# Mixers of the first two token tiles on shared weight loads, and half of the feed-forward weights narrowed by cast transfers inside device memory

## What is computed

```
u = rmsnorm(h); q, f, i, og, xp, ga, gb = split(u @ w_in)          # w_in: 1024 x 6656
o  = hgrn2(q, f, i)            # 8 heads, state 128 x 128 per head, carried along the tokens
ya = (rmsnorm_per_head(o) * sigmoid(og)) @ w_br_hgrn               # 1024 x 1024
yb = pool_mixer(xp) @ w_br_pool                                    # 4 trailing-mean windows, 512 x 1024
h  = h + (sigmoid(ga) * ya + sigmoid(gb) * yb) @ w_out             # 1024 x 1024
u  = rmsnorm(h)
h  = h + (silu(u @ w_ffn_gate) * (u @ w_ffn_up)) @ w_ffn_down      # 1024 x 2816, twice, and 2816 x 1024
return rmsnorm(h)[:, 16:]
```

## Time and profile before

| | |
|---|---|
| median of 3 runs | 2167.08 us (2166.81 to 2477.38) |
| profiled execution, its own time | 2170.29 us |
| its span on the slowest core, 5 | 2168.7 us (cores 2158.5 to 2168.7) |
| TensorE busy | 2088.9 us, 96% |
| VectorE, ScalarE, GpSimd busy | 1001.8, 1007.0, 574.0 us |
| mean granted TensorE clock | 0.985 to 0.987 of full |
| moved by DMA | 405.24 MB, mean 187 GB/s |

### The profile page before, as it was taken

The page is one execution under the profiler, slowest core; times in us unless marked ns, Lnnn a source line. Parts: engine busy times, 40 slices in busy tenths (PEclk is TensorE's granted clock), DMA queues, the critical chain, the costliest instruction groups (busy, mean ns, idle before and its releaser), DMA issues.

```text
span 2168.7 us, 38075 instructions; the slowest of 8 cores (2158.5 to 2168.7 us)
## 1 busy us (share of the span) xinstructions
PE 2088.9 (96%) x11476; PEld 1106.8 (51%) x11476; DVE 1001.8 (46%) x1756; ACT 1007.0 (46%) x1492; POOL 574.0 (26%) x671
## 2 busy tenths in 40 slices
PE   6777998999999999999999999999999999999997
PEld 3432554555555555555555555555555555554447
DVE  4644453447534742474246523662357235732223
ACT  4832763258415742464247623662358324731111
POOL 3121120001105251423243143314332414223300
PEclk9988999999999999999999999999999999999999
DMA  9999999887565666557555755575557555565577
GB/s 202 211 198 249 217 223 238 228 213 221 147 183 154 186 190 177 158 156 225 170 151 170 223 162 159 168 222 162 166 164 199 180 173 158 165 175 174 169 197 191
DMA packets 232789, 405.24 MB, mean 187 GB/s; under 512 B 24208, under 2 KB 66704, under 8 KB 232592
## 3 DMA queue, kind: packets, MB, share of 16 engines
q1 hardware_dynamic: 210080, 364.62, 57.6%
q0 software_dynamic: 20880, 36.32, 11.7%
q10 hardware_dynamic: 1632, 1.88, 0.4%
HBM read 385.94 MB, written 53.08 MB: 202 GB/s over the span
## 4 chain that ended last, share of the span: by engine, by line
PE 84%; DMA 12%; SPq 1%; issue 1%; DVE 1%; ACT 1%; POOL 0%; DVEq 0%; POOLq 0%; ACTq 0%
PE psa L496 75%; DMA wsc<-wr 6%; DMA wr<-wpk 5%; PE psa L661 5%; DMA wr<-wsc 1%; PE psa L782 1%; SPq L364 1%; PE psa L796 1%; PE psa L815 1%; PE psa L816 1%; PE psa L831 0%; DMA fa<-xT 0%; PE psa L620 0%; PE psa L601 0%; DVE ba L630 0%
## 5 line engine op out<-in xcount | busy, mean ns | idle before, releaser
L496 PE MATMUL psa<-ba,wr 128*128 128x456 bf16 (+2 forms) x8960 | 1776.7, 354 | 19.8 <-DVE ba L546 6.6
L496 PEld LDWEIGHTS psa<-ba,wr 128*128 128x128 bf16 x8960 | 868.1, 98 | 830.2 <-issue 40.6
L906 DVE TENSOR_TENSOR ba<-psa,fa 128x456 bf16<-128x456 f32 (+1 forms) x198 | 124.5, 631 | 250.8 <-PE psa L496 213.0
L905 ACT ACTIVATE fa<-psa 128x456 f32<-128x456 f32 (+1 forms) x198 | 107.1, 551 | 217.1 <-PE psa L496 185.1
L589 POOL TENSOR_TENSOR fa<-fa 128x456 f32<-128x456 f32 (+1 forms) x160 | 158.0, 996 | 161.8 <-DMA fa<-xT 76.9
L773 POOL TENSOR_TENSOR ba<-fa 128x456 bf16<-128x456 f32 (+1 forms) x48 | 61.1, 1272 | 480.7 <-ACT fa L756 257.9
L363 POOL DMA_DIRECT2D wr<-wpk x145 | 76.8, 535 | 373.8 <-DMA wsc<-wr 180.6
L661 PE MATMUL psa<-wr,ba 128*114 128x512 bf16 (+1 forms) x576 | 136.6, 384 | 3.0 <-DMA wr<-wpk 3.0
L765 DVE TENSOR_TENSOR_SCAN fa<-ba,fa 128x456 f32<-128x456 bf16 (+1 forms) x72 | 83.4, 1159 | 120.1 <-ACT fa L763 120.0
L866 POOL TENSOR_TENSOR fa<-fa 128x456 bf16<-128x456 f32 (+1 forms) x48 | 55.3, 1152 | 289.2 <-DVE fa L863 289.2
L863 DVE SCALAR_TENSOR_TENSOR fa<-fa,psa 128x456 f32<-128x456 f32 (+1 forms) x72 | 45.3, 629 | 165.9 <-PE psa L496 165.9
(11 more groups left out here) (84 smaller groups left out, 1767.2 us busy)
## 6 DMA issues: line engine op xcount, KB each, us to landing
wr<-wsc SPq DMA_DIRECT2D x1040, 256.0 KB, 3.0
wr<-wpk POOLq DMA_DIRECT2D x128, 256.0 KB, 14.3
wsc<-wr SPq DMA_DIRECT2D x128, 256.0 KB, 18.3
wr<-wsc SPq DMA_DIRECT2D x72, 192.0 KB, 2.8
fa<-xT SPq DMA_DIRECT2D x6, 1824.0 KB, 13.9
outT<-fa SPq DMA_DIRECT2D x6, 1824.0 KB, 11.0
wr<-wsc SPq DMA_DIRECT2D x72, 128.0 KB, 2.3
fa<-xT SPq DMA_DIRECT2D x2, 1840.0 KB, 13.2
```

Source lines behind the costliest of these rows:

```text
L496: last = e.matmul(ps[bank][:, 0:c1 - c0], lhsT=sl[0].ap(i * 128, (i + 1) * 128), rhs=s_.ap(c0, c1), start=(start and i == 0), stop=(stop a ...
L905: yield act(lambda e: e.activation(out=sg.ap(0, nt), in_=ps[bg][:, 0:nt], func=AF.Silu), [PS(bg)], [sg.rg(0, nt)], tset="S", banks=[bg])
L906: yield dve(lambda e: e.tensor_tensor(out=ACT[fc].ap(0, nt), in0=ps[bu][:, 0:nt], in1=sg.ap(0, nt), op=ALU.mult), [PS(bu), sg.rg(0, nt)], ...
```

## The change

- The first two tiles are one group. Heads go in the order (tile 0, head 0), (tile 1, head 0), (0, 1), (1, 1) and so on; the values, the pooling projection, the merge and `WO` are likewise done for both tiles on one load of each unit (`wkey`, `wdone`: tile 1 uses tile 0's slot and gives it back). Tile 1 thus has no mixer loads of its own. The feed-forward parts stay separate.
- Tile 1's mixer gets buffers of its own (`TWIN`) inside buffers of later stages: its `U` is `U2`, its values and outputs lie in `ACT`, its merged output in `VB`, and a fourth set of head buffers and the pooling scratch lie in the third residual buffer (`HX`). The load of tile 2's input therefore waits for the last head of tile 1, the first feed-forward part for tile 1's merge, tile 2's values for tile 1's `WO`.
- While the group's heads run there are two pairs of PSUM banks for the recurrence (3, 4 and 6, 7) and three dense banks; then banks 3 and 4 become dense.
- Every second feed-forward unit (`DD`, 34 of 68) is narrowed by one DMA from `wpk` straight to `wsc`, issued by GpSimd behind each load from the 19th on, until all 34 are out. In tile 0 these units are then loaded from `wsc` by SyncE and are not written back.
- `master` spawns both feed-forward parts behind the group's merge, then tile 2 and the others as before.

```
+DD = [u for u in range(NU) if WU[u][1] in ("fg", "fu", "fd")][1::2]
+DDI = 1
...
-        free_banks = {b: 0.0 for b in range(NDENSE)}
+        free_banks = {b: 0.0 for b in range(KA2)}
...
+        GROUP = [[(t, h) for h in range(8) for t in (0, 1)]] + [[(t, h) for h in range(8)] for t in range(2, n_tiles)]
+        def wkey(t, name):
+            return (0, name) if t == 1 else (t, name)
+
+        def wdone(t, keys):
+            return () if t == 0 else keys
...
-            if t == 0:
+            if t == 0 and u not in DD:
                 P.emit("pool", lambda e: e.dma_start(out=sbuf, in_=wpk[u, :, 0:n]), ...)
                 pend.append((slot, lambda: P.emit("sp", lambda e: e.dma_start(out=back, in_=sbuf), ...), nissue[0]))
+                if nload[0] % DDI == 0 and nload[0] > NSLOT and ndd[0] < len(DD):
+                    k = ndd[0]
+                    u2 = DD[k]
+                    n2 = WU[u2][4] * WU[u2][5]
+                    ndd[0] += 1
+                    P.emit("pool", lambda e: e.dma_start(out=wsc[u2, :, 0:n2], in_=wpk[u2, :, 0:n2]), w=[(("dr", u2), 0, 1)], sem=f"d{k}", inc=16, dma=True, dur=0.54, xfer=XL)
...
         def s_norm1(t):
-            if t == 1:
-                yield Gate(("hs", 0, 7))
+            if t == 2:
+                yield Gate(("hs", 1, 7))
+                yield Count(("pooled", 0), 4)
+                yield Count(("pooled", 1), 4)
...
+                if t == 2:
+                    yield Count(("res", 1), 8)
...
         def s_head(t, h):
-            s = HS[(h + 1) % HSN]
+            grp, n = HSEQ[(t, h)]
+            KB = KA2 if t < 2 and n % 2 else KA_
+            s = HS[n % 4] if t < 2 else HS[(n + 1) % HSN]
...
-            yield Lock("KA")
+            if t == 1:
+                yield Gate(("hs", 0, h))
+            yield Lock(f"KA{KB}")
...
-        def s_merge(t):
-            yield Count(("head", t), 8)
+        def s_merge(ts):
+            seq = [(t, j) for j in range(8) for t in ts]
+            if len(ts) > 1:
+                seq = sorted(seq, key=lambda x: (x[1] + GAP * x[0], x[0]))
+            yield Gate(("hs", 1, 6)) if len(ts) > 1 else Count(("head", ts[0]), 8)
...
         def s_ffn(t):
-            if t:
-                yield Gate(("downpe", t - 1))
+            yield Gate(("downpe", t - 1) if t else ("mixed", 1))
...
         def master():
+            yield Spawn(1, s_norm1(0))
+            yield Spawn(1, s_norm1(1))
+            yield Spawn(1, s_norm1(2))
+            yield Spawn(0, s_pool1(0))
+            yield Spawn(0, s_pool1(1))
+            yield Spawn(1, s_v([(0, 0), (0, 1), (1, 0), (1, 1)]))
+            for t, h in GROUP[0]:
+                yield Spawn(0, s_head(t, h))
+            yield Spawn(1, s_merge((0, 1)))
+            yield Spawn(5, s_ffn(0))
+            yield Spawn(5, s_ffn(1))
+            for t in range(2, n_tiles):
+                if t >= 3:
+                    yield Gate(("oproj", t - 2))
+                    yield Spawn(1, s_norm1(t))
+                yield Gate(("mixed", t - 1))
...
```

More of the change, by code:

```diff
@@ L24 @@
 LAG = 8
+GAP = 1.5
 PG = 7
@@ L268, in build_nc @@
         semnames += [f"{c}{i}" for c in "wvb" for i in range(NSLOT)]
+        semnames += [f"d{k}" for k in range(len(DD))]
         sems = {n: es.enter_context(nc.semaphore("s_" + n)) for n in semnames}
@@ L280, in build_nc @@
         NH = 3
-        H = [[FA.alloc(NTM) for _ in range(8)] for _ in range(NH)]
-        HALL = [Buf(fa_t, None, h[0].off, 8 * NTM) for h in H]
+        HALL = [FA.alloc(8 * NTM) for _ in range(NH)]
+        H = [[b.sub(j * NTM, NTM) for j in range(8)] for b in HALL]
         CF = FA.alloc(C_TOT)
@@ L524, in prologue @@
                 issue_load(0, u, s)
-            for i in range(HSN):
+            for i in range(HSN + 1):
                 g_(lambda e, i=i: e.memset(HS[i]["QI"].ap(128, 602), 0.0), [HS[i]["QI"].rg(128, 602)], dur=0.3)
@@ L644, in s_norm1 @@
                 yield Count(("u", t - 1), 8)
[L645 to L650, removed]
-            if t:
-                yield Count(("head", t - 1), 8)
-            for hf in range(2):
-                units = [(t, f"WI{hf}{i}") for i in range(4)]
+            yield from norm(t, H[t % NH], P_G1, MB(t).U, RSTD[0], "split" if t <= 1 else "sum" if t >= POOL_FROM else "mm",
+                            apply_gate=Gate(("ufree", 0 if t == 2 else t - 1)) if t >= 2 else None, out_flag="u")
@@ L655, in s_v, with fn @@
+        def s_v(parts):
+            for t, hf in parts:
+                nt = SIZES[t]
+                c = nt // 4
+                U_, V = MB(t).U, MB(t).V
+                yield Count(("u", t), 8)
+                if t == 2:
+                    yield Count(("res", 1), 8)
+                if t >= 3:
+                    yield Count(("head", t - 1), 8)
+                units = [wkey(t, f"WI{hf}{i}") for i in range(4)]
                 for ci in range(4):
                     b = yield Bank()
-                    def fn(e, sl, b=b, ci=ci):
+                    def fn(e, sl, b=b, ci=ci, c=c, U_=U_):
@@ L659, in fn @@
                         last = None
                         for kc in range(8):
-                            last = e.matmul(ps[b][0:c, 0:512], lhsT=U[kc].ap(ci * c, (ci + 1) * c),
+                            last = e.matmul(ps[b][0:c, 0:512], lhsT=U_[kc].ap(ci * c, (ci + 1) * c),
                                             rhs=sl[kc // 2].ap((kc % 2) * 512, (kc % 2) * 512 + 512), start=(kc == 0), stop=(kc == 7))
                         return last
-                    yield Op("pe", fn, [U[kc].rg(0, nt) for kc in range(8)], [PS(b)], 8 * 512 / 2400.0, units=units,
-                             done=units if ci == 3 else ())
+                    yield Op("pe", fn, [U_[kc].rg(0, nt) for kc in range(8)], [PS(b)], 8 * 512 / 2400.0, units=units,
+                             done=wdone(t, units) if ci == 3 else ())
@@ L704, in s_pool1 @@
                 yield dve(lambda e, sw=sw, xp=xp, g=g, w=w: e.scalar_tensor_tensor(
[L705 to L706 removed]
+                    out=YP[g].ap(0, nt), in0=xp.ap(16, end), scalar=-float(w), in1=sw.ap(16, end), op0=ALU.mult, op1=ALU.add),
+                    [xp.rg(16, end), sw.rg(16, end)], [YP[g].rg(0, nt)])
                 if t == 0:
[L708 removed]
+                    tmp = XTMP
                     yield dve(lambda e, sw=sw, g=g: e.tensor_tensor(out=tmp.ap(0, 16), in0=sw.ap(16, 32),
```

232 lines of the change are left out of this document (134 added, 98 removed).

## The result

The changed kernel takes 2191.61 us (2190.59 to 2193.24, 4 runs) against 2167.01 before: ratio 1.0115, 95% interval 1.0095 to 1.0134. It is slower by 1.15%: clear of no change, but under the 2% bound that the prediction set. 2137 us had been forecast, with a range of 2103 to 2176. In some eight-core executions the cores of a die run slow together; those are left out of all ratios, and of all medians from here on.

The account below looks back on a forecast made before the run. Before 360 us DMA was taken as the bound, afterwards TensorE; with the change, ScalarE in the joint heads. 2170.3 - 94.5 + 64 (56 + 4 + 4) = 2139.8 us, median 3.2 lower: 2137 us, range 2103 to 2176.

Parts of the forecast that it names:

- The two regimes: Kernel before: DMA engines full and TensorE with holes before 360 us; TensorE busy 1795.5 of 1800 us after.
- the 94.5 us that could be won: Before 360 us: 265.5 us of TensorE work in 360, so 94.5 us lost, all there is to win.
- the bound that DMA would give way to: Joint head stage of two tiles: ScalarE ends last, with 147 us of work; DMA is hidden there.
- the 0.84 of the forecast: Joint head stage: ScalarE occupancy, taken from tile 2's head stage, busy 79.8 of 95 us.
- my 1.62 us: DMA price of one narrowing load unit, taken also for one transfer inside device memory.
- my upper value of 2.56: Upper DMA price in us of one transfer inside device memory: the load and write-back it stands for.
- Rival 3: Transfers inside device memory are slow: gain gone at 3.7 us each, 2229 us at 5.5; chance 0.07.
- 147/0.84 = 175 us from 22 on ... heads end at 200 us: Joint head stage: 147 us of ScalarE work at 0.84 occupancy, 3 us of start lost, end at 200 us.
- rival 2: Heads run as tile 0's did, ScalarE at 0.68: end at 241 us, 2178 us in all; chance 0.12.
- Moved waits that I cost at nothing: Tile 2's input waits for the last head, its values for tile 1's `WO`; tile 0's feed-forward part covers both.
- Later the feed-forward parts run one tile behind: Later tiles: tile 3's load waits for tile 0's store; a queued feed-forward part of 102 us covers it, at no cost.
- Rival 4: Gain given back later: tile 3's input or single feed-forward units late, 25 us, 2162 us; chance 0.13.

Follow-up runs that it names:

- a_no_dd: The changed kernel with `DD` empty, so no transfers inside device memory: 1.0161 times the kernel before, 2213.78 us, on the second kind of chip.
- a_act2: The changed kernel with the output gate's Tanh computed twice in each of the first two tiles' 16 heads: 1.0129 times the kernel before.
- a_skew: The changed kernel with tile 1's heads one and a half places behind tile 0's, merge gates swapped: 1.0093 times the kernel before, 2188.6 us.
- x2_late_2: The changed kernel with tile 2's input load and norm held back behind the merge, second run: 1.0054 times the kernel before, 2190.7 us.
- a_nolag: The changed kernel with tile 2's values and heads held back until tile 0's down projection: 1.0042 times the kernel before, median 2174.2 us.

## Why the prediction was wrong

**What held.** The two regimes, the 94.5 us that could be won, and the bound that DMA would give way to: TensorE does not wait for a narrowing load from 60 us to the end of the merge, and a_no_dd shows that the head stage ignores DMA. ScalarE as the next bound fits a_act2. Behind the heads TensorE was full (95.00 of 95 us in 245 to 340), without a DMA wait. ScalarE was busy 117.3 of 140 us in 60 to 200, the 0.84 of the forecast; TensorE 0.86 there, not 0.75.

Two readings were off without effect on the sum. In the earlier trace rows TensorE is at 9 from the eighth slice to the last but one, and the DMA engines are for seven slices, not eight. And a head has 16 small matmuls, as the prediction priced them, not the 24 named ahead of it.

**The price of a transfer inside device memory.** From 180 to 220 us only GpSimd's queue moves data:

```profile
q0 software_dynamic: 2380, 5.06, 101.3%
```

That is 40/5.06 = 7.9 us per MB, 2.1 us per unit, for narrowing loads and transfers inside device memory mixed; no row has the transfers alone. In 20 to 180 us the queue was given 40 loads and 31 transfers. If the loads cost between my 1.62 us and the 1.9 us that their own share of the engines gives in the earlier trace rows (72.8% of 160 us for 16.18 MB), a transfer cost 2.3 to 2.6 us, an estimate, at my upper value of 2.56. It cost nothing, as this was not the bound. Rival 3 did not come. The estimate of 2.2 us by the Trainium skill's page HBM Reference, Specifications (TRN2), lies between the 2.1 us of the mixture and this; no run measured a transfer by itself.

**First failed step: "147/0.84 = 175 us from 22 on ... heads end at 200 us".** The occupancy was wrong, not the work. ScalarE was busy 157.8 us in 22 to 230 instead of 147, but 7.8 of the 10.8 more are constants and first merge products, which the forecast had set aside and which run inside the stage all the same; the heads' own surplus is about what 3 table loads over twice tile 0's 18 take, 3.8 us. The occupancy was 0.84 in 60 to 200 as forecast, but 0.54 in 22 to 60 and 0.67 in 200 to 230. Priced at 0.84, the empty start costs 14 us, of which 3 were allowed for, the thin end 6 and the 10.8 us of work 13: together, less those 3, about the 29 us. I took the occupancy of a stage in full flow for one that starts empty; the joint stage can't flow until both tiles' values exist, at 102 us. a_skew shows one part of that, 7 of the 29 us; the others were not taken apart by an experiment. The end lies between the forecast's 200 and rival 2's 241 us.

**Second failed step: "Moved waits that I cost at nothing".** Tile 2's input: I named tile 0's feed-forward part as cover. But cover must stand in the list ahead of the wait. TensorE's list had the norm's product ahead of the merge, and SyncE's had the load ahead of 19 write-backs; TensorE stood still for 8.4 us. By x2_late_2 its removal alone leaves 1 us at the end, with nolag 4 us.

**Third, and the largest: "Later the feed-forward parts run one tile behind ... another feed-forward part is queued then and covers".** I asked whether TensorE would have work, and it had. I did not ask what the lag puts beside the feed-forward part on the other engines. The next input comes only after a store, so the next tile's first norm falls into the middle of a feed-forward part, and its eight products on VectorE stand ahead of the one product that the down projection needs. Behind 360 us 27 us were given back. The seven waits on L984 (12.4 us) and the two late units around 565 us (5.4 us) are 17.8 of them; a_nolag takes back 15 in all, and the cause of the rest stays open. Rival 4 had the mechanism, "the gain is given back later", at 0.13 and 25 us, but as late inputs and units; what came late was mostly VectorE's product.

**The sum redone.** 2137 + (88.4 - 64) + 26.8 = 2188 us, against 2191.6. This takes the measured span apart and is no check of it; the 3.4 us left are the 3.2 by which the median had been put below the profiled execution, which did not recur. Either miss alone would have stayed in the range; I gave rivals 2 and 4 their chances as alternatives, though nothing keeps them from coming together.

## What to carry to other kernels

When two stages are fused to share loads, add up what the other engines do in the fused stage: the filler that ran beside each of them is gone, and the stage starts empty, so the occupancy of a stage in full flow is too good for it. A wait that moves costs whatever stands behind it in each in-order list, also when TensorE has other work in plenty. And a schedule that is shifted by one tile at the start stays shifted in every tile; read what the shift puts side by side on VectorE, and look first for the one gate that undoes it.

## What the hardware showed that was not expected

Between chips the kernel before differs by 0.4 to 0.5% (medians of 2167 to 2169 and of 2178 us), while the changed kernel differs by 0.15% at most (2189.0 and 2191.6 on the first kind, 2192.0 us on the second). No run tells why. Eight products of 128 x 460 on VectorE (L674) took 10.4 us, 1.3 us each, where the median of that line over the changed kernel's span is 0.688 us. GpSimd started nine products of 1.16 to 1.36 us in the same 12 us. The Trainium skill's page SBUF — State Buffer, SBUF: two separate sides, has the two engines lock one pair of ports for a whole instruction when VectorE reads two operands from SBUF and GpSimd reads SBUF too; the near equal pace of both fits that, but no run here took GpSimd's products away.
